# Two attention steps entered together: regrouping the window-attention units of a streaming encoder layer on one core

## The chip, the core and the metric

The kernel runs on 1 core of one Trainium2 chip. The metric is the device time of the whole program in microseconds (us), the median of a few runs. TensorE (PE) does matrix products and transposes, VectorE (DVE) and ScalarE (ACT) do elementwise work, SyncE (SP) issues nearly all DMAs from one queue in program order, and GpSimd (POOL) has almost nothing to do here.

## What is computed

One layer for a prompt of 1024 frames and a "sample" of 32 new frames: 1056 columns of tokens, cut below into eight tiles of 128 (numbers 0 to 7) and the sample (number 8, `TT`).

```python
h = rms_norm(x, norm_pre)
qa, ka, va, ga, qb, kb, vb, gb, qc, kc, vc, gc = split(h @ w_in)
oa = stick_breaking(qa, ka, va)                       # A: 12 heads, whole past
ob = band_attention(qb, kb, vb, ALiBi bias, sinks)    # B: 12 q heads, 4 kv heads, own chunk + 2 before
oc = band_attention(qc, kc, vc, relative bias)        # C: 8 heads, own chunk + 8 before
o = concat(oa * silu(ga), ob * silu(gb), oc * silu(gc)) @ w_out
x = x + rms_norm(o, norm_post)
```

## The kernel before

**Products and ticks.** `h @ w_in` is made in tiles of 128 output columns. The weights of a tile arrive in four pieces of 512 columns; ACT and DVE split each piece into a high and a low part (`w_hi`, `w_lo`), and PE takes three products of split operands (L1162, L1163, L1164, 352 token columns each). A tile is 12 groups (4 pieces by 3 token groups) of 12 matmuls. One such group is one "tick" of the plans.

**Units.** The attention is cut into 16 units of two heads: six of kind A (0 to 5), four of kind C (6 to 9), six of kind B (10 to 15; 10 to 12 share one pair of key/value heads, 13 to 15 the other). Each unit has a slot of ticks: unit 10 starts at tick 504, 11 at 528, 12 at 552 (twice as long), 13 at 600, 14 at 624, 15 at 648; the products end at tick 660, and then the output product with `w_out` (L1369 to L1375) begins.

**Steps of a B unit.** A unit handles its token tiles in five steps (`BAND_STEPS`). A step goes: scores on PE (`band_scores`, L1265) into one of two pairs of PSUM banks ("sets"); bias and row minimum on DVE (L1836), exponentials on ACT (L1540), reciprocal and scaling on DVE (L1843, L1848); the weights are transposed in blocks of 32 by DVE (L2006), sent to DRAM by SP (`part_weights`, L945) and loaded back whole (`load_weights`, L956); PE multiplies them with the values (`band_values`, L1344) into bank 7; ACT keeps the sums (L1660) and DVE multiplies them by the gate (L1770). The sample's step, and every step of the last unit 15, go another way for the transpose: PE turns them (`band_turn`, L1277) and ACT copies the result out (L1525 to L1530). Weights of a step lie in one of `B_FLIGHT` buffers `b_s`. `GROUP_END` says after which steps the sums in bank 7 are kept.

**Order.** Each engine has a plan, a list of (tick, task), sorted by the tick with Python's stable sort; entries with the same tick stay in the order in which they were appended, and products are appended first. An engine does its list in order and waits on semaphores. The ticks come from small functions: `step_starts` (scores), `values_at`, `turn_at`, `chain_at` (DVE and ACT work of a step), `cache_at`, `bias_at`. The lines that append to PE's plan:

```python
    plan = [(float(t), "product", t // 12 + 1, t % 12) for t in range(TICKS)]
...
            plan.append((START[u][i], "scores", u, i))
            if not by_blocks(u, i):
                plan.append((turn_at(u, i), "turn", u, i))
        plan += [(values_at(u, n), "values", u, n) for n in range(STEPS[kind])]
```

An "entry" below is a place where PE leaves the products for attention work and comes back; a "run" is a stretch of one kind of matmul in it (scores, values or turns). The trace has two records for each fp32 matmul of the attention, so four score matmuls are "x8" there.

Of the kernel before, what the change touches and what calls it, by code (L numbers as in the profile page):

```python
# [10 lines left out]
P = 128  # L11
# [3 lines left out]
TOK = SEQ + DEC  # L15
# [6 lines left out]
NA, NB, NC = H_A // 2, H_BKV // 2, H_C // 2  # L22
# [60 lines left out]
           step_of((6, PAST, 384), (4, PAST, 128)), step_of((5, PAST, 256), (1, 0, 256)), step_of((4, 0, PAST)), step_of((5, 0, PAST)),  # L83
           step_of((6, 0, PAST)), step_of((TT, 0, PAST + DEC))]

BAND_STEPS = {"c": ((4, 1), (5,), (3, 2), (6,), (7, 0), (TT,)), "b": ((0, 1), (2, 3), (4, 5), (6, 7), (TT,))}
GROUP_END = {"a": (3, 8, 9), "c": (1, 3, 5), "b": (1, 3, 4)}
STEPS = {"a": len(A_STEPS), "c": len(BAND_STEPS["c"]), "b": len(BAND_STEPS["b"])}
STEP0 = [sum(STEPS[UNITS[v][0]] for v in range(u)) for u in range(NU + 1)]
HEADS = 2 * (TT + 1)  # L90
# [55 lines left out]

def chain_at(u, i):

    return START[u][i] + (SECOND if UNITS[u][0] == "a" and i % 2 else 0)


def next_start(u, i):

    if i < len(START[u]):
        return START[u][i]
    if UNITS[u][0] == "b" and u + 1 < NU:
        return START[u + 1][i - len(START[u])]
    return START[u][-1] + 1.4 * (i + 1 - len(START[u]))
# [2 lines left out]

FLIGHT = 4
C_FLIGHT = 2
B_FLIGHT = 3
LAST_A, LAST_C = NA - 1, NA + NC - 1


# [7 lines left out]

def by_blocks(u, i):

    return u + 1 < NU and (UNITS[u][0] == "a" or i + 1 < STEPS[UNITS[u][0]])


def turn_at(u, i):

    kind = UNITS[u][0]
    if kind != "b":
        return chain_at(u, i) + {"a": 5, "c": 4}[kind]
    return next_start(u, i + 1) + 0.01


def values_at(u, n):

    kind = UNITS[u][0]
    if kind == "a":
        if n + FLIGHT < STEPS["a"]:
            return START[u][n + FLIGHT] - 0.02
        if n + 1 == STEPS["a"] and u < LAST_A:
            return START[u + 1][2] + 3.5
        if u < LAST_A:
            return START[u + 1][n + FLIGHT - STEPS["a"]] - 0.02
        return chain_at(u, n) + 14.6
    if kind == "c":  # L200
        if n + C_FLIGHT < STEPS["c"]:
            return START[u][n + C_FLIGHT] - 0.02
# [47 lines left out]

def pace(u, i):

    return 2.0 if UNITS[u][0] == "c" else min(2.0, 0.75 * (next_start(u, i + 1) - START[u][i]))


def at_piece(r):
# [151 lines left out]
def cache_at(u):  # L408
    return SLOT[u] + 3.0


def dve_plan():
# [27 lines left out]
def sp_plan():  # L440
    plan = [(piece_at(T, q), "piece", T, q) for T in range(1, TILES) for q in range(4)]
    for u in range(NU):
        if NEW_KV[u]:
            k, v = 12 * TILE_OF["k", u], 12 * TILE_OF["v", u]
            plan += [(k + 3.0, "store_keys", u, 0), (v + 0.6, "part_values", u, 0), (v + 8.0, "load_values", u, 0),
                     (v + 12.0, "store_values", u, 0), (cache_at(u), "cache_keys", u, 0), (SLOT[u] + (14.5 if 0 < u < NA else 10.5 if u == NA else 6.0), "cache_values", u, 0)]
# [73 lines left out]
def build(nc, x_prompt, x_sample, cache_a_k, cache_a_v, cache_b_k, cache_b_v, cache_c_k, cache_c_v,  # L520
# [3 lines left out]
    with ctx:  # L524
# [45 lines left out]
        c_bias = work[:, 3072:4352].rearrange("p (h c) -> p h c", h=2)  # L570


        oT = arena[:, 9376:9376 + TOK]

        B_HEAD = 512 + 32
        B_COLS = B_HEAD + 512
        b_s = [arena[:, 10432 + (B_COLS + 2) * i:10432 + (B_COLS + 2) * (i + 1)] for i in range(B_FLIGHT)]

        b_bias = [arena[:, c:c + 2 * n].rearrange("p (h c) -> p h c", h=2)[:, :, 0:2 * P] for c, n in ((7584, 2 * P), (8096, 672))]
# [107 lines left out]

        def part_no(u, i):

            return STEP0[u] - max(0, u - NA) + i + 1  # L690

        def parted_by(u, i):

# [112 lines left out]
        def turned_of(u, i, h):  # L806

            if UNITS[u][0] == "b":
                c = 1 + B_HEAD * h + (P if i == 0 and by_blocks(u, i) else 0)
# [53 lines left out]
        def cache_blocks(u):  # L863
            return 1 if UNITS[u][0] == "b" else 4
# [14 lines left out]
        def _(sp):  # L879
# [26 lines left out]

            def cached_values(u):
                c = P * UNITS[u][1]
                sp.dma_start(vc[:, 0:cache_blocks(u), :],
                             caches_of(u)[1][0, 0].rearrange("(b p) h d -> p b (h d)", p=P)[:, :, c:c + P]).then_inc(vc_in, 16)  # L910

            def outputs_of(u, which):
# [179 lines left out]
            for _, what, u, n in sp_plan():  # L1092
# [23 lines left out]
                elif what == "cache_keys":  # L1116

                    if u:
                        sp.wait_ge(z_ready, Z_COUNT[u - 1, STEPS[UNITS[u - 1][0]] - 1])
                    cached_keys(u)  # L1120
                elif what == "cache_values":
                    if u:
                        sp.wait_ge(pv_done, STEP0[u])
                    cached_values(u)
                elif what == "bias":
                    bias_load(u)
# [15 lines left out]
        def _(pe):  # L1142
# [139 lines left out]
            def value_rows(u, blk, h):  # L1282
                cached, own, keys = blk
                hp = slice(DH * h, DH * h + DH)

                return vc[:, cached, hp] if own is None else v_nat[KV[u] % 2][:, own, hp]

            def o_free(u, n):
                ends = GROUP_END[UNITS[u][0]]
# [157 lines left out]
        def _(act):  # L1447
# [58 lines left out]
            def turned_out(u, i):  # L1506
# [12 lines left out]
                            last.then_inc(set_free[0], 1)  # L1519
                else:  # L1520
                    z = ps[:, 512 * zb:512 * zb + 1024].rearrange("p (h k) -> p h k", h=2)
                    if i + 1 < STEPS["b"]:
# [601 lines left out]
```

## Time and profile before

| | |
|---|---|
| median of 3 runs | 1967.0 us (1963.57 to 1967.22) |
| profiled execution, its own time | 1968.51 us |
| its span | 1966.8 us |
| PE busy | 1919.5 us, 98% of the span |
| DVE busy | 1243.7 us, 63% |
| ACT busy | 657.5 us, 33% |
| mean granted clock of TensorE | 0.991 of full speed |

A busy share of 98% says that PE always has a matmul in flight, not that each of them runs at its best pitch: matmuls overlap, and what an interruption costs is seen from the distance between their starts.

### The profile page before, as it was taken

Reading aid. Unit: us, or ns where it says so; the run is one execution under the profiler, and the core shown is the slowest. Engines: PE = TensorE matmul, PEld = TensorE weight load, DVE = VectorE, ACT = ScalarE, POOL = GpSimd, SP = SyncE. Lnnn points to the kernel's source line nnn. Section 1 sums busy time; section 2 is a strip of 40 time slices with the busy share of each in tenths; the row PEclk is TensorE's granted clock in tenths of the full one; section 3 lists DMA queues with packets and bytes.
Section 4 is the critical chain, followed back from the end, with each engine's and each line's share of the span. In section 5 each row is a group of like instructions: output and inputs, shape, how many; then the busy total and the mean of one; then the engine's idle time right before and its main releaser. Section 6 shows DMA issues by size and latency. Waiting matters only on the chain.

```text
span 1966.8 us, 31027 instructions
## 1 busy us (share of the span) xinstructions
PE 1919.5 (98%) x12604; PEld 1758.3 (89%) x12604; DVE 1243.7 (63%) x2228; ACT 657.5 (33%) x1239; POOL 21.9 (1%) x66
## 2 busy tenths in 40 slices
PE   6999999999999999999999999999999999999996
PEld 5999999999999999899999999989999988888875
DVE  7358687787768778354445344555435567766898
ACT  7133343343433333122222122322223354344432
POOL 3000000000000000000000000000000000000000
PEclk9999999999999999999999999999999999999998
DMA  6447767776776767576656576555445576534476
GB/s 241 115 119 140 159 150 160 160 149 147 148 155 149 161 148 159 120 144 148 139 118 154 128 147 125 125 133 120 105 100 126 127 274 228 195 108 154 151 250 242
DMA packets 882215, 301.05 MB, mean 153 GB/s; under 512 B 618472, under 2 KB 845560, under 8 KB 880600
## 3 DMA queue, kind: packets, MB, share of 16 engines
q1 hardware_dynamic: 881912, 296.90, 61.8%
q8 instruction: 99, 1.62, 0.3%
q0 software_dynamic: 160, 2.17, 0.3%
q14 instruction: 44, 0.36, 0.1%
HBM read 210.45 MB, written 91.75 MB: 154 GB/s over the span
## 4 chain that ended last, share of the span: by engine, by line
PE 91%; DVE 5%; DMA 1%; issue 1%; SPq 1%; ACT 0%; DVEq 0%; POOL 0%
PE ps L1162 22%; PE ps L1163 21%; PE ps L1164 21%; PE ps L1373 4%; PE ps L1374 4%; PE ps L1375 4%; PE ps L1265 3%; PE ps L1344 3%; PE ps L1226 3%; PE ps L1315 3%; DVE arena L1691 1%; DVE act_lo L1698 1%; PE ps L1370 1%; PE ps L1369 1%; DMA b_out<-in_w_out_dram 0%
## 5 line engine op out<-in xcount | busy, mean ns | idle before, releaser
L1162 PE MATMUL ps<-act_hi,w_hi 128*128 128x352 f32 x2688 | 879.2, 327 | 3.9 <-DVE arena L1730 3.9
L1163 PE MATMUL ps<-act_lo,w_hi 128*128 128x352 f32 x2688 | 864.0, 321 | 0.0
L1164 PE MATMUL ps<-act_hi,w_lo 128*128 128x352 f32 x2688 | 863.8, 321 | 0.0
L1162 PEld LDWEIGHTS ps<-act_hi,w_hi 128*128 128x128 f32 x2688 | 505.6, 188 | 21.0 <-issue 18.1
L1163 PEld LDWEIGHTS ps<-act_lo,w_hi 128*128 128x128 f32 x2688 | 506.5, 188 | 0.0
L1164 PEld LDWEIGHTS ps<-act_hi,w_lo 128*128 128x128 f32 x2688 | 505.3, 188 | 0.0
L1473 ACT ACTIVATE w_hi<-w_raw 128x512 fp32r<-128x512 f32 x224 | 139.1, 623 | 343.5 <-DMA w_raw<-in_w_in_dram 343.2
L1706 DVE TENSOR_TENSOR w_lo<-w_raw,w_hi 128x512 fp32r<-128x512 f32 x224 | 150.4, 673 | 55.1 <-ACT w_hi L1473 54.8
L1540 ACT ACTIVATE arena<-arena,small 128x257 f32<-128x257 f32 (+6 forms) x180 | 101.2, 565 | 219.2 <-DVE small L1836 219.2
L2006 DVE STREAM_TRANSPOSE arena<-arena 128x1024 f32<-128x1024 f32 (+4 forms) x100 | 132.5, 1325 | 50.3 <-ACT arena L1638 49.5
L1638 ACT ACTIVATE arena<-arena 128x1024 f32<-128x1024 f32 (+1 forms) x60 | 61.0, 1017 | 250.2 <-DVE arena L1813 250.2
L1373 PE MATMUL ps<-w_hi,l_hi 128*128 128x512 f32 x280 | 110.1, 393 | 8.4 <-DVE w_lo L1890 5.5
L1375 PE MATMUL ps<-w_hi,l_lo 128*128 128x512 f32 x280 | 109.7, 392 | 0.0
L1374 PE MATMUL ps<-w_lo,l_hi 128*128 128x512 f32 x280 | 109.6, 391 | 0.0
L1836 DVE CUSTOM_DVE_ANT_0 arena<-ps,arena 128x640 f32<-128x640 f32 (+5 forms) x72 | 44.0, 660 | 93.6 <-PE ps L1265 84.2
L1789 DVE TENSOR_TENSOR arena<-ps,arena 128x1024 f32<-128x1024 f32 (+1 forms) x60 | 70.2, 1171 | 30.9 <-ACT arena L1634 30.8
L1730 DVE COPY arena<-ps 128x352 f32<-128x352 f32 x84 | 42.9, 514 | 62.0 <-PE ps L1164 61.9
L1801 DVE TENSOR_TENSOR_SCAN arena<-arena 128x512 f32<-128x512 f32 (+4 forms) x102 | 79.5, 833 | 0.8
L1548 ACT ACTIVATE w_hi<-w_raw 128x512 fp32r<-128x512 f32 x70 | 44.0, 629 | 104.1 <-DVE w_raw L1873 89.2
L1634 ACT ACTIVATE arena<-arena 128x1024 f32<-128x1024 f32 (+1 forms) x60 | 61.1, 1019 | 52.2 <-DVE arena L2016 52.2
L1630 ACT ACTIVATE arena<-ps 128x1024 f32<-128x1024 f32 (+1 forms) x60 | 58.5, 975 | 54.4 <-PE ps L1243 46.6
L1739 DVE TENSOR_SCALAR arena<-ps 128x352 f32<-128x352 f32 x48 | 25.1, 522 | 75.6 <-PE ps L1164 75.6
(173 smaller groups left out, 2086.1 us busy)
## 6 DMA issues: line engine op xcount, KB each, us to landing
w_raw<-in_w_in_dram SPq DMA_DIRECT2D x176, 256.0 KB, 3.4
weight_scratch<-arena SPq DMA_DIRECT2D x216, 128.0 KB, 3.4
arena<-weight_scratch SPq DMA_DIRECT2D x54, 512.0 KB, 4.4
b_out<-in_w_out_dram SPq DMA_DIRECT2D x80, 256.0 KB, 3.4
w_raw<-in_w_out_dram SPq DMA_DIRECT2D x70, 256.0 KB, 2.7
w_raw<-in_w_in_dram SPq DMA_DIRECT2D x96, 128.0 KB, 3.1
weight_scratch<-arena SPq DMA_DIRECT2D x80, 132.0 KB, 4.1
arena<-weight_scratch SPq DMA_DIRECT2D x40, 256.0 KB, 3.4
```

Source lines behind the costliest of these rows:

```text
L1162: mm(bank(g, GN), wh, ah, start=(k == 0), stop=False)
L1163: mm(bank(g, GN), wh, al, start=False, stop=False)
L1164: last = mm(bank(g, GN), wl, ah, start=False, stop=(k == KT - 1))
L1373: mm(out, th, wh, start=first, stop=False)
L1374: mm(out, th, wl, start=False, stop=False)
L1375: last = mm(out, tl, wh, start=False, stop=end)
L1473: fn(w_hi[:, q, :], w_raw[:, q, :], ACT.Copy).then_inc(hi_made, 1)
L1540: fn(s, s, ACT.Exp, bias=neg_max[0:rows_of(m), t:t + 1], scale=-1.0, accum_out=row_sum[0:rows_of(m), t:t + 1]).then_inc(p_exp, 1)
L1706: v.tensor_tensor(w_lo[:, slot, :], w_raw[:, slot, :], w_hi[:, slot, :].bitcast(F32), ALU.subtract).then_inc(lo_made, 1)
L1789: v.tensor_tensor(both, z, both, ALU.max).then_inc(sp_ready, 1)
L1801: v.tensor_tensor_scan(along, along, along, 0.0 if newest else carry[:, 2 * m - 8 + h:2 * m - 7 + h], ALU.add, ALU.max).then_inc(sum_ready, 1)
L2006: v.transpose(s, s).then_inc(wt_blocks, 1)
```

## The change

The B units 10 to 14 take the sample's step first and alone; the steps (0, 1) and (2, 3) start one behind the other, then (4, 5) and (6, 7). The second step of such a pair has its DVE and ACT work planned 2.7 ticks behind the first. Values are taken two steps at a time, with a fourth score buffer for it. The sums are kept after the steps 0, 2 and 4. Unit 15 keeps its single steps, but the sample is first there too. To make room, `oT` and `b_s` move, the cached values of B get their own place, one bias table lies in `mask_c`, and the loads of cached keys and values come earlier.

```diff
-BAND_STEPS = {"c": ((4, 1), (5,), (3, 2), (6,), (7, 0), (TT,)), "b": ((0, 1), (2, 3), (4, 5), (6, 7), (TT,))}
-GROUP_END = {"a": (3, 8, 9), "c": (1, 3, 5), "b": (1, 3, 4)}
+BAND_STEPS = {"c": ((4, 1), (5,), (3, 2), (6,), (7, 0), (TT,)), "b": ((TT,), (0, 1), (2, 3), (4, 5), (6, 7))}
+GROUP_END = {"a": (3, 8, 9), "c": (1, 3, 5), "b": (0, 2, 4)}
...
+def in_pairs(u):
+
+    return UNITS[u][0] == "b" and u + 1 < NU
...
-    if (kind, i, r) == ("b", 0, 0):
-        begin = 6
-    if kind == "b" and end > 24:
-
-        return [SLOT[u] + 0.5] + [SLOT[u] + 5.5 + (end - 5) * x // (n - 1) for x in range(n - 1)]
+    if in_pairs(u):
+        first, second, third = (6.5, 10.7, 16.5) if u == B0 else (0.5, 5.0, 20.0 if end > 24 else 12.0)
+        return [SLOT[u] + x for x in (first, second, second + 0.01, third, third + 0.01)]
     return [SLOT[u] + begin + (end - begin) * x // n + 0.5 for x in range(n)]
...
 def chain_at(u, i):
 
+    if in_pairs(u):
+        return START[u][i] + (2.7 if i in (2, 4) else 0)
     return START[u][i] + (SECOND if UNITS[u][0] == "a" and i % 2 else 0)
...
-B_FLIGHT = 3
+B_FLIGHT = 4
...
+    if in_pairs(u):
+        return START[u][1] - 0.04
     return next_start(u, i + 1) + 0.01
...
-    return next_start(u, n + (B_FLIGHT if n < 3 and by_blocks(u, n) else 2)) - 0.02
+    if in_pairs(u):
+        return (START[u][3] if n == 0 else START[u + 1][0 if n < 3 else 1]) - 0.02
+    return next_start(u, n + 2) - 0.02
...
-    return START[u - 2][-1] + 1.2
+    return START[u - 2][-1] + 4
```

**PE inside unit 11.** Names: `ps` is PSUM, `arena` the buffer with keys, queries, weights and values; scores are L1265 before and L1286 after, values L1344 and L1365, turns L1277 and L1298. Each line of dots stands for product groups of 12 rows (five at each place before; four, one, six and one after) or for the second half of a turn. Before, from the unit's third step to the entry that begins the next unit:

```order
L1265 MATMUL ps<-arena 128x256 x4
...
L1344 MATMUL ps<-arena 64x128 x6
L1265 MATMUL ps<-arena 128x256 x4
...
L1344 MATMUL ps<-arena 64x128 x8
L1265 MATMUL ps<-arena 32x128 x2
L1265 MATMUL ps<-arena 32x32 x2
...
L1344 MATMUL ps<-arena 64x128 x16
L1265 MATMUL ps<-arena 128x128 x2
```

After, the whole unit from its first entry:

```order
L1365 MATMUL ps<-arena 64x128 x14
L1286 MATMUL ps<-arena 32x128 x2
L1286 MATMUL ps<-arena 32x32 x2
...
L1298 MATMUL ps<-ident,arena 128x32
L1298 MATMUL ps<-ident,arena 32x32
...
L1365 MATMUL ps<-arena 64x128 x16
...
L1286 MATMUL ps<-arena 128x128 x2
L1286 MATMUL ps<-arena 128x256 x6
...
L1365 MATMUL ps<-arena 64x32 x4
...
L1286 MATMUL ps<-arena 128x256 x8
```

The scores of two steps now stand together, and so do the values; but a group of 12 products stands between the values at the second place and the scores there, and again at the third place, because these starts are whole ticks (5.0 and 12.0) and the product of the same tick is sorted ahead of the scores, the values at a hundredth of a tick less ahead of both.

**SP where unit 10 ends.** `weight_scratch` is the DRAM copy of the weights, `w_raw` a piece of `w_in`, `in_alibi_dram` and `in_attn_sinks_dram` the bias and sinks of unit 12. Before:

```order
L945 DMA weight_scratch<-arena 32x33x32 x4
L890 DMA w_raw<-in_w_in_dram 128x4x64 x2
L992 DMA arena<-in_alibi_dram 128x256
L993 DMA small<-in_attn_sinks_dram 128x1
L992 DMA arena<-in_alibi_dram 128x256
L993 DMA small<-in_attn_sinks_dram 128x1
L956 DMA arena<-weight_scratch 128x4x128 x2
```

After:

```order
L964 DMA weight_scratch<-arena 32x33x32 x4
L1011 DMA arena<-in_alibi_dram 128x256
L1012 DMA small<-in_attn_sinks_dram 128x1
L1011 DMA arena<-in_alibi_dram 128x256
L1012 DMA small<-in_attn_sinks_dram 128x1
L909 DMA w_raw<-in_w_in_dram 128x4x64 x2
L975 DMA arena<-weight_scratch 128x4x128 x2
L964 DMA weight_scratch<-arena 32x33x32 x4
L909 DMA w_raw<-in_w_in_dram 128x4x64 x2
L975 DMA arena<-weight_scratch 128x4x128 x2
```

In both the last row is the load of unit 10's last blocked step; before, PE wants it at tick 528.48, 2.4 ticks behind the load's place in the plan (526.1); after, at tick 532.98, 4.2 ticks behind its place (528.81).

**PE at the end of unit 15.** Before, the last three entries (the dots are one product group, then the second half of the turn and 18 rows of the output product):

```order
L1344 MATMUL ps<-arena 64x128 x8
L1265 MATMUL ps<-arena 32x128 x2
L1265 MATMUL ps<-arena 32x32 x2
L1277 MATMUL ps<-ident,arena 128x128 x8
...
L1344 MATMUL ps<-arena 64x128 x8
L1277 MATMUL ps<-ident,arena 128x32
...
L1344 MATMUL ps<-arena 64x32 x4
```

After:

```order
L1365 MATMUL ps<-arena 64x128 x8
L1286 MATMUL ps<-arena 128x256 x4
L1298 MATMUL ps<-ident,arena 128x128 x8
...
L1365 MATMUL ps<-arena 64x128 x8
L1298 MATMUL ps<-ident,arena 128x128 x8
...
L1365 MATMUL ps<-arena 64x128 x8
```

The last step is now the full pair of tiles (6, 7) instead of the sample, with one product group and eight value matmuls between its scores and its turn.

## Rows read from the trace of the kernel before

**Rows 1.** The page: span; busy time of PE, share, instructions.

```profile
span 1966.8 us, 31027 instructions
PE 1919.5 (98%) x12604; PEld 1758.3 (89%) x12604; DVE 1243.7 (63%) x2228; ACT 657.5 (33%) x1239; POOL 21.9 (1%) x66
```

**Rows 2.** Timeline of PE, last values of unit 10: start, us, idle before and releaser.

```profile
1296.50 1.10 PE L1344 MATMUL ps<-arena 128*64 128x128 f32 x16 [2.87 <-DMA arena<-weight_scratch]
```

**Rows 3.** Chain that ended last, in order of time: start, us, what.

```profile
1291.61 4.85 DMA arena<-weight_scratch
```

**Rows 4.** Stretches: length, busy of PE, PEld, DVE, ACT, POOL; granted clock; DMA.

```profile
1296.50:1301.20 4.70, 4.70 (x34) 3.79 (x35) 1.58 (x10) 1.67 (x10) 0.00 (x0) 0.64 0.03 7
```

**Rows 5.** Timeline of PE, an entry with scores alone.

```profile
1476.34 0.32 PE L1163 MATMUL ps<-act_lo,w_hi 128*128 128x352 f32 x1
1476.49 0.32 PE L1164 MATMUL ps<-act_hi,w_lo 128*128 128x352 f32 x1
1476.75 1.14 PE L1265 MATMUL ps<-arena 64*128 64x256 f32 x8
1477.81 0.43 PE L1162 MATMUL ps<-act_hi,w_hi 128*128 128x352 f32 x1
1478.08 0.32 PE L1163 MATMUL ps<-act_lo,w_hi 128*128 128x352 f32 x1
```

**Rows 6.** Timeline of PE, two entries with values.

```profile
1454.53 1.98 PE L1344 MATMUL ps<-arena 128*64 128x128 f32 x32
1456.44 0.93 PE L1265 MATMUL ps<-arena 64*128 64x128 f32 x8
1457.30 0.36 PE L1277 MATMUL ps<-ident,arena 32*128 32x32 f32 x4
...
1499.27 1.10 PE L1344 MATMUL ps<-arena 128*64 128x128 f32 x16
1500.30 0.47 PE L1265 MATMUL ps<-arena 64*32 64x128 f32 x8
```

**Rows 7.** Timeline of PE, scores of two A steps in one run.

```profile
336.63 2.00 PE L1226 MATMUL ps<-arena 64*128 64x512 f32 x12
338.56 0.51 PE L1243 MATMUL ps<-mask_b,ident_b 128*128 128x128 bf16 x6
```

**Rows 8.** Timeline of PE, end of unit 15 and the output product's first wait.

```profile
1598.38 1.09 PE L1277 MATMUL ps<-ident,arena 128*128 128x128 f32 x8
1599.23 0.40 PE L1162 MATMUL ps<-act_hi,w_hi 128*128 128x352 f32 x1
1601.32 1.10 PE L1344 MATMUL ps<-arena 128*64 128x128 f32 x16
1602.35 0.36 PE L1277 MATMUL ps<-ident,arena 32*128 32x32 f32 x4
...
1613.98 0.47 PE L1373 MATMUL ps<-w_hi,l_hi 128*128 128x512 f32 x1 [0.92 <-DVE w_lo L1890]
```

**Rows 9.** Timelines of PE, ACT and DVE after the scores of tiles 6 and 7 in unit 15.

```profile
1590.19 1.09 PE L1277 MATMUL ps<-ident,arena 128*128 128x128 f32 x8
...
1592.77 0.52 ACT L1540 ACTIVATE arena<-arena,small 128x257 f32<-128x257 f32 x1
...
1593.91 0.17 DVE L1843 RECIPROCAL small<-small 128x2 f32<-128x2 f32 x1 [0.40 <-ACT arena L1540]
...
1595.08 0.62 DVE L1848 TENSOR_SCALAR arena<-arena,small 128x256 f32<-128x256 f32 x2
```

**Rows 10.** A late tile copy (timeline of PE; stretch behind it), then DVE in unit 11.

```profile
817.72 0.63 PE L1162 MATMUL ps<-act_hi,w_hi 128*128 128x352 f32 x1 [3.94 <-DVE arena L1730]
...
817.70:822.00 4.30, 4.28 (x14) 3.92 (x16) 2.03 (x4) 0.00 (x0) 0.00 (x0) 0.50 0.87 128
...
1309.68 0.17 DVE L1827 COPY arena<-small 128x2 f32<-128x2 f32 x1 [4.76 <-PE ps L1265]
...
1314.20 1.28 DVE L2006 STREAM_TRANSPOSE arena<-arena 128x1056 f32<-128x1056 f32 x1
...
1319.54 0.53 DVE L1730 COPY arena<-ps 128x352 f32<-128x352 f32 x1 [3.49 <-PE ps L1164]
```

More of the change, by code:

```diff
@@ L176, in by_blocks @@
 def by_blocks(u, i):
-    return u + 1 < NU and (UNITS[u][0] == "a" or i + 1 < STEPS[UNITS[u][0]])
+    kind = UNITS[u][0]
+    return u + 1 < NU and (kind == "a" or BAND_STEPS[kind][i][0] < TT)
 def turn_at(u, i):
@@ L251, in pace @@
 def pace(u, i):
-    return 2.0 if UNITS[u][0] == "c" else min(2.0, 0.75 * (next_start(u, i + 1) - START[u][i]))
+    return 2.0 if UNITS[u][0] == "c" or in_pairs(u) else min(2.0, 0.75 * (next_start(u, i + 1) - START[u][i]))
 def at_piece(r):
@@ L404, in bias_at, with cache_values_at @@
         return unit_end_at(NA + NC - 1) + 0.3 + 0.1 * r
-    return START[u - 2][-1] + 1.2
+    return START[u - 2][-1] + 4
 def cache_at(u):
+    if UNITS[u][0] == "b":
+        return SLOT[u] - (9 if u == B0 else 20)
     return SLOT[u] + 3.0
+def cache_values_at(u):
+    if UNITS[u][0] == "b":
+        return cache_at(u) + 0.2
+    return SLOT[u] + (14.5 if 0 < u < NA else 10.5 if u == NA else 6.0)
 def dve_plan():
@@ L445, in sp_plan @@
             plan += [(k + 3.0, "store_keys", u, 0), (v + 0.6, "part_values", u, 0), (v + 8.0, "load_values", u, 0),
-                     (v + 12.0, "store_values", u, 0), (cache_at(u), "cache_keys", u, 0), (SLOT[u] + (14.5 if 0 < u < NA else 10.5 if u == NA else 6.0), "cache_values", u, 0)]
+                     (v + 12.0, "store_values", u, 0), (cache_at(u), "cache_keys", u, 0), (cache_values_at(u), "cache_values", u, 0)]
         if UNITS[u][0] != "a":
@@ L570, in build @@
         c_bias = work[:, 3072:4352].rearrange("p (h c) -> p h c", h=2)
-        oT = arena[:, 9376:9376 + TOK]
+        oT = arena[:, 8896:8896 + TOK]
+        vc_b = arena[:, 8768:8896].rearrange("p (b c) -> p b c", b=1)
         B_HEAD = 512 + 32
         B_COLS = B_HEAD + 512
-        b_s = [arena[:, 10432 + (B_COLS + 2) * i:10432 + (B_COLS + 2) * (i + 1)] for i in range(B_FLIGHT)]
-        b_bias = [arena[:, c:c + 2 * n].rearrange("p (h c) -> p h c", h=2)[:, :, 0:2 * P] for c, n in ((7584, 2 * P), (8096, 672))]
+        b_s = [arena[:, 9952 + (B_COLS + 2) * i:9952 + (B_COLS + 2) * (i + 1)] for i in range(B_FLIGHT)]
+        b_bias = [t.rearrange("p (h c) -> p h c", h=2) for t in (arena[:, 7584:8096], mask_c[:, :])]
         x_t = [arena[:, o:o + D] for o in (1152, 1152 + D, 1152 + 2 * D, 1152 + 4 * D + D // 2)]
@@ L688, in part_no @@
         def part_no(u, i):
-            return STEP0[u] - max(0, u - NA) + i + 1
+            return STEP0[u] - max(0, u - NA) + i + (UNITS[u][0] != "b")
         def parted_by(u, i):
@@ L808, in turned_of @@
             if UNITS[u][0] == "b":
-                c = 1 + B_HEAD * h + (P if i == 0 and by_blocks(u, i) else 0)
+                c = 1 + B_HEAD * h + (P if i == 1 and by_blocks(u, i) else 0)
                 return b_s[(STEP0[u] + i) % B_FLIGHT][:, c:1 + B_HEAD * h + 512]
@@ L908, in cached_values @@
                 c = P * UNITS[u][1]
-                sp.dma_start(vc[:, 0:cache_blocks(u), :],
+                sp.dma_start((vc_b if UNITS[u][0] == "b" else vc)[:, 0:cache_blocks(u), :],
                              caches_of(u)[1][0, 0].rearrange("(b p) h d -> p b (h d)", p=P)[:, :, c:c + P]).then_inc(vc_in, 16)
@@ L1118, in _ @@
                     if u:
-                        sp.wait_ge(z_ready, Z_COUNT[u - 1, STEPS[UNITS[u - 1][0]] - 1])
+                        sp.wait_ge(z_ready, Z_COUNT[u - 1, 0 if in_pairs(u - 1) else STEPS[UNITS[u - 1][0]] - 1])
                     cached_keys(u)
                 elif what == "cache_values":
-                    if u:
-                        sp.wait_ge(pv_done, STEP0[u])
+                    if u == B0:
+                        sp.wait_ge(z_ready, Z_COUNT[u - 1, STEPS["c"] - 1])
+                    elif u:
+                        sp.wait_ge(pv_done, STEP0[u - 1] + 1 if in_pairs(u - 1) else STEP0[u])
                     cached_values(u)
@@ L1284, in value_rows @@
                 hp = slice(DH * h, DH * h + DH)
-                return vc[:, cached, hp] if own is None else v_nat[KV[u] % 2][:, own, hp]
+                return (vc_b if UNITS[u][0] == "b" else vc)[:, cached, hp] if own is None else v_nat[KV[u] % 2][:, own, hp]
             def o_free(u, n):
@@ L1521, in turned_out @@
                     z = ps[:, 512 * zb:512 * zb + 1024].rearrange("p (h k) -> p h k", h=2)
-                    if i + 1 < STEPS["b"]:
+                    if BAND_STEPS["b"][i][0] < TT:
                         nk = sum(keys_of(u, m) for m in BAND_STEPS["b"][i])
```

## The prediction

> **What bounds the kernel now.** I read the page first: PE is busy for 98% of the span [rows 1], so a change pays only where PE waits, runs at the low clock, or starts its matmuls further apart than it could. Next I read PE's timeline through the B units, looking at two things: the rows that carry a wait, and the distances between starts at each entry. From unit 10 to the last product there is a single wait: the last blocked values of unit 10 stand 2.87 us for the DMA that brings their weights back from DRAM [rows 2]. The chain of waits shows that DMA in flight for 4.85 us [rows 3], and the stretch behind the wait runs at a mean granted clock of 0.64, that is partly at 1.2 GHz instead of 2.4 [rows 4]. Everywhere else in the B units PE always has work, and what is lost is lost at the joints: the product behind an entry starts late, and so does each run of another kind.
>
> **What a joint costs.** Products start 0.15 to 0.16 us apart. An entry with scores alone has 0.26 us from the last product to the first score, and 0.27 us from the first product behind it to the second [rows 5]: about 0.21 us for each entry, whatever is in it. Inside, a run has a fixed part. Eight records of scores of 256 columns take 1477.81 - 1476.75 = 1.06 us [rows 5]; the unit's first step has half of them at 128 columns and takes 0.86 us [rows 6]. So 512 columns are 0.20 us, 2048 are 0.80, and 0.26 is fixed; had 512 columns taken 0.21, it would be 0.22. I take 0.24. Values: 32 records take 1.91 us and 16 take 1.03 [rows 6], 0.055 each, which leaves 0.15 fixed. Do two steps behind one another share the fixed part? For values, yes: the 32 records are two steps. For scores the nearest row is of kind A: two steps of 2048 columns each take 1.93 us together [rows 7], 0.20 less than twice 1.06, so they shared nearly one fixed part.
>
> TensorEngine Tiling (Array Packing) of the Trainium skill, section Key Properties, says that changing the tiling mode drains TensorE. Scores are 64*128 in these rows, values 128*64 and products 128*128, so by that rule each change of kind has a price and each merge of equal kinds saves one; the rows give the price, the page none.
>
> **The change, part by part.**
>
> *Entries.* The name of the change promises three for five, which by 0.21 us would be two in each of five units. The order says otherwise. In units 11 to 14 the second and third starts are whole ticks, so a product group slips between the values and the scores: each of these units has five entries, as before. Unit 10 starts at 6.5, 10.7 and 16.5 and does get fewer. Counted from the start of the B units to the output product, entries go from 32 to 30: 2 x 0.21 = 0.4 us.
>
> *Runs.* In the same stretch score runs go from 30 to 20 and value runs from 25 to 20; turns stay at 10. That is 10 x 0.24 + 5 x 0.15 = 2.4 + 0.75 = 3.15 us. Entries and runs together 3.5 us. Bounds: 3.0 with all fixed parts at the low reading; 1.2 if scores of two steps don't share theirs; 4.4 with 0.33 for a score run ([rows 7] read with the slope of [rows 6]).
>
> *The wait at the end of unit 10.* Before, PE comes for these weights at tick 528.48, 2.4 ticks behind the load's place in SP's plan; a product group is 12 starts 0.16 apart, 1.92 us, so that is some 4.6 us, less than the 4.85 us of the DMA alone, and SP is late besides, having the bias of unit 12 ahead of it. After, the same load has 4.2 ticks (8.1 us) and two entries of about 2 us each besides; the bias stands ahead of an earlier load. The work that has to be done in this time: the second chain of the pair (bias, exponentials, scaling, transpose) is as long as in unit 11, 1315.48 - 1309.68 = 5.8 us [rows 10], and is already in the plan's 2.7 ticks plus 3. I expect no wait: 2.87 us gone, and with it the low clock: 4.70 x (1 - 0.64) = 1.69 us. Together 4.56 us. If a wait remains, the cover lost is that of SP's queue; kept whole, the gain here is nothing. All other pairs have nine or more ticks from load to use.
>
> *The fourth buffer and the moved loads.* B's cached keys and values are now asked for 9 and 20 ticks ahead of the slot, behind scores that are long done; nobody waits for them. No DMA is added, and the pieces of `w_in` behind them in SP's queue are asked for nine ticks ahead of their use. I put this at nothing.
>
> *The last unit.* Its last step is now a full one. Take the scores' end as zero. In the same step before, the turn of the previous step began at 1590.19, ACT's first exponential at +2.6, the reciprocals at +3.7, the last scaled block at +5.5 [rows 9]. PE comes for it at 1602.35 - 1598.38 = +4.0 (turn, one product group, values) [rows 8], needs 0.85 us of turning (1599.23 - 1598.38), and must wait in the middle of it: it ends at about +6.0 and not +4.8, so 1.2 us are lost. What hides it: 11 us later PE waited 0.92 us for a split piece of `w_out` [rows 8], made by DVE from DMAs that were released by the last product and not by this turn. So 0.92 of the 1.2 is taken from that wait, and 0.3 us remain. The turn and the values of the step (about 1.2 us more than the sample's) stand behind the last product now instead of before it; that only moves them. Bounds: 0, and +1.2 if the later wait moves along.
>
> **The sum**, against the profiled execution's own 1968.51 us: 1968.51 - 3.5 - 4.56 + 0.3 = 1960.75. The median of the runs is 1.5 us lower than that execution, and part of this may be a smaller wait in unit 10, which can't be gained twice; I take 1960.5 us. A measurement of this kernel tells about 0.2% (3.9 us) from no change, so the bound of "faster" is 1963.1.
>
> **The rivals.**
>
> *A. The wait stays or moves.* The loads of both pairs go through one SP queue with four transposed stores, bias and pieces ahead of them, and a DMA there has taken 4.85 us [rows 3]. If the values of the pair wait as long as before, or if the median run had little of this wait, only the joints are gained: 1967.0 - 3.5 + 0.3 = 1963.8, which is "same"; with half of it, 1962 to 1965. For it: the highest and the lowest run of before are 3.7 us apart, so something like this comes and goes. Against it: 3.5 us more plan time than before. Chance 0.22.
>
> *B. The merged runs save nothing.* If scores in another pair of banks start as a new run: 1.2 us of joints, 1968.51 - 1.2 - 4.56 + 0.3 = 1963.1. The row of the A scores [rows 7] speaks against it. Chance 0.06.
>
> *C. Slower: the pair's work on DVE delays the copies of the products.* DVE does two chains back to back, and the copy that frees the product banks (L1730, L1739) stands behind them in its queue. What that costs is seen once, elsewhere: 3.94 us of waiting and then a granted clock of 0.50 over 4.3 us [rows 10], 3.94 + 2.15 = 6.1 us at least. In unit 11 a chain is 5.8 us including 1.25 for the gate; DVE then stood idle 3.49 us before the copy [rows 10], and PE needs the bank three product groups later, 5.8 us. A second chain of 4.5 us fits into 9.3. It decides once DVE is more than 4.8 us later than this: then one such wait gives 1967, two give 1973 or more. The copies of the next tile fall right behind the second pair start in units 11, 13 and 14. Chance 0.10.
>
> *D. The joints cost nothing.* If the distance between starts came from the columns alone, merging would save nothing and the time would be 1968.51 - 4.56 + 0.3 = 1964.25. The fixed parts in the rows of the B entries [rows 5, 6] stand against it. Chance 0.02.
>
> TensorE: Matmul & The Clock Gate of the Trainium skill, section Back-to-back issue gap, gives the gap of a matmul by its columns, with no term for a change of kind; that is rival D, and the trace does not agree.
>
> **How the numbers follow.** Forecast 0.60, its own range 1957.5 to 1963. Rival A 0.22 (a quarter of it below 1963.1), B 0.06 (half), C 0.10 (a tenth of it a single short wait, which is "same"), D 0.02. Faster: 0.60 + 0.05 + 0.03 = 0.68; same: 0.17 + 0.03 + 0.01 + 0.02 = 0.23; slower 0.09. The range for 8 in 10 goes from 1957 (joints at 4.4 us, and the tail's wait fully absorbed, 2 us for chance) to 1966.5, which takes in A and B.
>
> **What the profile after will show.** Right: no wait of values for the weights' DMA near the end of unit 10 and a granted clock of 1.00 through the B units; two steps of scores in about 1.9 us instead of twice 1.06; five entries still in each of the units 11 to 14; a turn in unit 15 that stops for about 1.2 us for DVE's scaling, with a shorter first wait of the output product. Wrong: a PE wait on DVE's tile copies or on ACT's copy of the sample's turn in the B units, a wait on `weight_scratch` at another place, or score runs of 2.1 us.

## The result and the profile after

The kernel after takes 1975.7 us (median of 6 runs, 1972.49 to 1978.09), the kernel before 1965.24 us (6 runs, 1963.57 to 1967.22). The ratio is 1.0049 (95% interval 1.0039 to 1.0059): 0.5% slower, outside the range of the forecast. The profiled execution took 1976.8 us.

The page after, where [rows 1] stood for before:

```profile
span 1975.1 us, 31027 instructions
PE 1918.6 (97%) x12604; PEld 1762.2 (89%) x12604; DVE 1241.2 (63%) x2228; ACT 657.1 (33%) x1239; POOL 21.8 (1%) x66
```

PE, DVE and ACT are busy for about as long as before (1919.5, 1243.7, 657.5 us). The 8.3 us by which the span grew are idle time of PE and low clock, less what the joints saved. PE's timeline from the first B unit to the output product has these waits (start, us, instruction, idle before and releaser; before, this stretch has the single one of [rows 2] and the small ones of the output product):

```profile
1304.29 1.10 PE L1365 MATMUL ps<-arena 128*64 128x128 f32 x16 [1.58 <-DMA arena<-weight_scratch]
...
1351.43 0.47 PE L1286 MATMUL ps<-arena 64*32 64x128 f32 x8 [1.34 <-issue]
...
1431.90 0.66 PE L1183 MATMUL ps<-act_hi,w_hi 128*128 128x352 f32 x1 [3.53 <-DVE arena L1748]
...
1517.53 0.75 PE L1286 MATMUL ps<-arena 64*32 64x128 f32 x8 [4.07 <-issue]
...
1576.96 0.47 PE L1286 MATMUL ps<-arena 64*32 64x128 f32 x8 [1.31 <-issue]
...
1611.51 0.44 PE L1298 MATMUL ps<-ident,arena 128*128 128x128 f32 x2 [0.27 <-DVE arena L1869]
...
1612.48 0.88 PE L1298 MATMUL ps<-ident,arena 128*128 128x128 f32 x6 [0.54 <-DVE arena L1869]
```

The 64*32 scores at 1351, 1517 and 1577 us are the sample's step, the first of units 12, 14 and 15. "<-issue" says only that the profile found no semaphore for the wait. The stretches behind the two long waits (same columns as [rows 4]):

```profile
1517.53:1524.00 6.47, 6.47 (x28) 6.41 (x29) 2.62 (x10) 2.57 (x7) 0.00 (x0) 0.51 0.36 72
1431.90:1435.20 3.30, 3.30 (x12) 3.30 (x12) 1.55 (x3) 0.61 (x1) 0.00 (x0) 0.52 0.59 89
```

**The balance.** Waits: 1.58 + 1.34 + 3.53 + 4.07 + 1.31 + 0.27 + 0.54 = 12.64 us. Low clock: 6.47 x 0.49 + 3.30 x 0.48 = 4.75 us. Before, the same stretch lost 2.87 + 1.69 = 4.56 us [rows 2, 4]. That makes 12.83 us more. From unit 10's first scores to the first output product is 1602.64 - 1250.80 = 351.84 us before and 1613.11 - 1251.70 = 361.41 after: 9.57 more, and 10.2 for equal work, since the full step's values (0.67 us longer than the sample's) now stand behind that product. So 12.83 - 10.2 = 2.6 us were saved at the joints. Unit 10 begins 0.90 us later than before, and the stretch behind the first output product is 2.2 us shorter: 0.90 + 9.57 - 2.2 = 8.3.

**What the sample's scores wait for.** SP, then ACT, then DVE, ahead of 1351.43:

```profile
1335.87 0.96 SPq L1011 DMA_DIRECT2D mask_c<-in_alibi_dram  x1
...
1339.19 0.93 SPq L975 DMA_DIRECT2D arena<-weight_scratch  x2
1340.22 4.64 SPq L964 DMA_DIRECT2D weight_scratch<-arena  x4
1344.90 2.27 SPq L909 DMA_DIRECT2D w_raw<-in_w_in_dram  x2
...
1349.11 0.63 ACT L1494 ACTIVATE w_hi<-w_raw 128x512 fp32r<-128x512 f32 x1 [12.63 <-DMA w_raw<-in_w_in_dram]
...
1342.71 0.53 DVE L1760 TENSOR_SCALAR arena<-ps 128x352 f32<-128x352 f32 x1 [2.98 <-PE ps L1185]
1349.77 0.69 DVE L1727 TENSOR_TENSOR w_lo<-w_raw,w_hi 128x512 fp32r<-128x512 f32 x1 [6.53 <-ACT w_hi L1494]
1350.38 0.95 DVE L1760 TENSOR_SCALAR arena<-ps 128x352 f32<-128x352 f32 x2
```

Read it backwards. The scores start as soon as DVE has copied the last two thirds of the query tile (L1760, 1350.38 to 1351.33). These copies stand behind the split of a piece of `w_in` (L1727). The split waits for ACT's, ACT's for the DMA of the piece, and SP asked for the piece at 1344.90, behind the four stores of the pair's second step (4.64 us), the load of the pair's first step, and the four bias loads. DVE is idle for 6.53 us, ACT for 12.63. The other two waits of this kind have the same rows (the piece comes to ACT at 1515.21 and 1574.64). At 1431.90 it is the copies of a value tile (L1748, transposes) that stand behind the split, and with them PE's next product bank:

```profile
1425.55 0.51 DVE L1748 STREAM_TRANSPOSE arena<-ps 128x352 f32<-128x352 f32 x1
1430.69 0.69 DVE L1727 TENSOR_TENSOR w_lo<-w_raw,w_hi 128x512 fp32r<-128x512 f32 x1 [4.64 <-ACT w_hi L1494]
1431.30 0.97 DVE L1748 STREAM_TRANSPOSE arena<-ps 128x352 f32<-128x352 f32 x2
```

In the kernel before, SP at the same place has one step's stores, then the piece (timeline of SP):

```profile
1338.65 3.38 SPq L945 DMA_DIRECT2D weight_scratch<-arena  x4
1342.07 2.36 SPq L890 DMA_DIRECT2D w_raw<-in_w_in_dram  x2
1345.61 0.92 SPq L956 DMA_DIRECT2D arena<-weight_scratch  x2
```

The two kernels reach the same tick at different times, so these starts can't be compared as they stand. Unit 12's first entry is a common mark. It begins with values, at 1348.33 us after and, before, here:

```profile
1352.96 1.98 PE L1344 MATMUL ps<-arena 128*64 128x128 f32 x32
```

Before, the piece is asked for 1352.96 - 1342.07 = 10.9 us ahead of that entry; after, 1348.33 - 1344.90 = 3.4 us ahead. It is 7.5 us later.

**Unit 10's wait.** The chain of waits of the kernel after that ends in the 1.58 us:

```profile
1291.85 0.51 SPq L975
...
1293.01 0.44 SPq L964
...
1294.72 2.05 SPq L964
...
1296.82 3.69 DMA weight_scratch<-arena
...
1300.53 0.37 SPq L975
...
1300.93 3.31 DMA arena<-weight_scratch
...
1304.29 1.10 PE ps L1365 x16
```

From one load's issue to the next (1291.85 to 1300.53) 8.7 us pass: four stores, their landing, the load. A pair needs this twice, one behind the other, and then the landing. No engine's arithmetic is in that chain.

### The profile page after: what moved, and what is told of

It reads as the page before. It is cut to its first block, busy times and chain, and to the rows that moved or that the text cites. A ratio compares the mean times of both kernels' runs of the same rounds, so it can differ in the third digit from the quotient of the medians.

```text
span 1975.1 us, 31027 instructions
## 1 busy us (share of the span) xinstructions
PE 1918.6 (97%) x12604; PEld 1762.2 (89%) x12604; DVE 1241.2 (63%) x2228; ACT 657.1 (33%) x1239; POOL 21.8 (1%) x66
## 4 chain that ended last, share of the span: by engine, by line
PE 87%; DVE 6%; SPq 2%; DMA 2%; issue 2%; ACT 1%; DVEq 0%; POOL 0%; ACTq 0%
PE ps L1183 21%; PE ps L1184 20%; PE ps L1185 20%; PE ps L1394 4%; PE ps L1396 4%; PE ps L1395 4%; PE ps L1286 3%; PE ps L1365 3%; PE ps L1247 3%; PE ps L1336 3%; SPq L964 1%; PE ps L1391 1%; PE ps L1390 1%; DMA weight_scratch<-arena 1%; PE ps L1173 0%
## 5 line engine op out<-in xcount | busy, mean ns | idle before, releaser
L1727 DVE TENSOR_TENSOR w_lo<-w_raw,w_hi 128x512 fp32r<-128x512 f32 x224 | 150.8, 674 | 118.5 <-ACT w_hi L1494 118.2
L1561 ACT ACTIVATE arena<-arena,small 128x257 f32<-128x257 f32 (+7 forms) x180 | 101.3, 565 | 220.7 <-DVE small L1857 220.7
L1760 DVE TENSOR_SCALAR arena<-ps 128x352 f32<-128x352 f32 x48 | 24.8, 522 | 73.8 <-PE ps L1185 73.7
```

Of the source, the lines that this page charges most:

```text
L1561: fn(s, s, ACT.Exp, bias=neg_max[0:rows_of(m), t:t + 1], scale=-1.0, accum_out=row_sum[0:rows_of(m), t:t + 1]).then_inc(p_exp, 1)
L1727: v.tensor_tensor(w_lo[:, slot, :], w_raw[:, slot, :], w_hi[:, slot, :].bitcast(F32), ALU.subtract).then_inc(lo_made, 1)
```

## The experiments

All ran beside the kernel before on the same chip; a ratio is to that one, with its 95% interval.

**1. The piece ahead of the second step's stores**

```diff
+late = 0.4 if in_pairs(u) and i == 4 else 0
-plan += [(at, "part_weights", u, i), (at + (2.6 if u >= B0 else 4.0), "load_weights", u, i)]
+plan += [(at + late, "part_weights", u, i), (at + (2.6 if u >= B0 else 4.0), "load_weights", u, i)]
```

> The changed kernel, with the stores of each pair's second step planned 0.4 ticks later in SP's queue, so that the next piece of w_in is issued ahead of them. Queue theory (the four stores hold SP, the piece of w_in lands late, DVE's split waits for it and the copies of the query tile queue behind the split): the three waits of the sample's scores in units 12, 14 and 15 (1.34, 4.07, 1.31 us) and the low clock behind the second (3.4 us of loss) go, the time falls from 1975.7 to about 1966; the waits at 1304 us (1.58) and 1432 us (3.53) stay. Rival, DVE overworked: DVE does the same work, the waits stay, 1975. Rival, transfers collide: the same bytes move, the piece is as late as before, 1973 to 1976.

Measured: 1972.61 us, ratio 1.003 (1.0018 to 1.0042). The three waits of the sample's scores are gone, but waits of 3.79 us for unit 10's weights and 3.38 us at a value tile stand in the trace, both with a stretch of low clock behind them. The sample's turns in units 12 and 14 wait too, 0.42 and 1.40 us, so the time stayed 6.6 us above the expectation. The pieces were what the sample's scores waited for; what stands behind the pieces is late now.

**2. DVE's copies ahead of the late split**

```diff
-plan = [(piece_at(T, q) + 4.2, "lo", T, q) for T in range(1, TILES) for q in range(4)]
+plan = [(piece_at(T, q) + (5.95 if q == 1 and 12 * (T - 2) >= SLOT[B0] else 4.2), "lo", T, q) for T in range(1, TILES) for q in range(4)]
```

> The changed kernel, SP's queue as it is; on DVE the split of the second piece of each tile stands behind the three copies of the tile before, from unit 10 on. Queue theory: the piece is as late as before, but nothing queues behind it, so the three waits of the sample's scores go, about 1966 us. DVE overworked: the copies come when the chains are done, the waits stay, 1975. If the late piece itself were what PE lacks, a wait on w_lo would take their place and the time would stay near 1975.

Measured: 1967.37 us, ratio 0.9998 (0.9989 to 1.0008). This one number gives back 8.3 us by the medians. SP's list is that of the kernel after, and yet the waits at 1351, 1431, 1517 and 1577 us are gone or at 0.20 us; two turns of the sample wait instead, 0.32 and 0.59 us, since the split is later still. Left is the wait for unit 10's weights:

```profile
1306.10 1.97 PE L1365 MATMUL ps<-arena 128*64 128x128 f32 x16 [4.03 <-DMA arena<-weight_scratch]
```

**3. The cached loads later**

```diff
-        return SLOT[u] - (9 if u == B0 else 20)
+        return SLOT[u] - 9
```

> The changed kernel, with the cached keys and values of unit 13 asked for 9 ticks ahead of the slot instead of 20. If these five DMAs, right behind the eight that store new keys, make the piece of w_in in unit 12 late, the wait of 3.53 us at 1432 us and the low clock behind it (1.7 us) go: 1970.5. If the wait comes from the chains of the pair alone, it stays: 1975.7. The three waits of the sample's scores stay in both cases.

Measured: 1974.45 us, ratio 1.0034 (1.0021 to 1.0046). The wait at the value tile fell from 3.53 to 1.30 us, the sample's waits stayed (1.68, 4.39 and 0.49 us). The clock behind it was at 1.00, where the kernel after has 3.30 us at 0.52. So the moved loads, which I had put at nothing, were about 2.2 us of that one wait and the 1.6 us of low clock behind it. The total fell by only 1.3 us, inside the intervals; unit 10's wait was 3.43 us in this profile, against 1.58 in that of the kernel after.

**4. The kernel before, with its bias loads behind the load of the weights**

```diff
-    return START[u - 2][-1] + 1.2
+    return START[u - 2][-1] + 2.0
```

> The kernel before, with only the bias load of each B unit 0.8 ticks later, so that in unit 10 it stands behind the load of the last weights in SP's queue. If that wait (2.87 us, and 1.7 us of low clock behind it) is SP's lateness, the load goes out 1.9 us earlier, the wait shrinks to about 1 us and the clock stays up: 1.9 to 3.6 us faster than before, 1962 to 1963.5. If the DMA's own time sets it, 1965.2 as before.

Measured: 1963.14 us, ratio 0.9982 (0.9973 to 0.9991). No wait is left in the B units. Unit 10's wait of [rows 2] came from four small loads (1.9 us of issue) ahead of the load, and one number in the kernel before takes it away. The change promised this gain by other means and didn't get it.

**5. The pairing alone undone**

```diff
+        if u > B0:
+            step = (SLOT_LEN[u] - 5.0) / 4
+            return [SLOT[u] + 0.5] + [SLOT[u] + 4.98 + step * x for x in range(4)]
...
-        return START[u][i] + (2.7 if i in (2, 4) else 0)
+        return START[u][i] + (2.7 if i in (2, 4) and u == B0 else 0)
```

> The kernel after, with the pairing alone undone in units 11 to 14: the sample's step stays alone and first and the buffers stay as they are, but the four full steps start one at a time, 4.75 ticks apart (10.75 in unit 12), and their DVE and ACT work isn't shifted. Theory (SP's queue): the stores of two steps stand behind one another on SP only because the steps are paired. Spread out, the stores leave room for the pieces of w_in, so the three waits of the sample's scores (0.47 to 1.34, 4.07, 1.31 us in the kernel after) shrink to less than a third, with the low clock at 1517 us; the price is 8 more score runs, 8 x 0.24 = 1.9 us. About 1975.7 - 6.7 - 3.4 + 1.9 = 1967.5 us. Rival (the sample's place): it is the sample's step at the head of the unit that is wrong, since it needs the last of the three tile copies half a tick behind the last product; then the three waits stay and the time is 1975.7 + 1.9 = 1977.6 us.

Measured: 1965.35 us, ratio 0.9996 (0.9987 to 1.0005). The three waits and the one at 1431 us are gone, though the sample is first in its unit as in the kernel after. Unit 10, whose pairs this run keeps, still waits 2.51 us for its weights. SP's timeline before unit 12 shows why the others are gone: the piece now stands behind the stores of one step, at 1337.42, 10.6 us ahead of the unit's first entry (1348.06 in this run), and not behind two rounds, at 1344.90. The copies don't wait.

```profile
1334.03 3.34 SPq L967 DMA_DIRECT2D weight_scratch<-arena  x4
1337.42 2.27 SPq L912 DMA_DIRECT2D w_raw<-in_w_in_dram  x2
1340.41 0.92 SPq L978 DMA_DIRECT2D arena<-weight_scratch  x2
1341.38 1.06 SPq L912 DMA_DIRECT2D w_raw<-in_w_in_dram  x2
1343.38 3.56 SPq L967 DMA_DIRECT2D weight_scratch<-arena  x4
```

The rival, the sample's place by itself, is out, and so are the moved buffers, which this run keeps.

**6 and 7. The change mended, and then without ties.** Number 6 is number 2 with `bias_at` at +9 instead of +4. Number 7 adds

```diff
-        first, second, third = (6.5, 10.7, 16.5) if u == B0 else (0.5, 5.0, 20.0 if end > 24 else 12.0)
+        first, second, third = (6.5, 10.7, 16.5) if u == B0 else (0.5, 4.98, 19.98 if end > 24 else 11.98)
```

> The kernel after with two edits of DVE's and SP's order: the split of the second piece planned behind the three tile copies (as in e2_copies_first), and the bias loads asked for 5 ticks later (START[u - 2][-1] + 9), which takes them out of the chain of stores and loads at the end of unit 10. Theory: SP's chain there becomes shorter by the four bias loads, 1.3 + 3.3 = 3 to 4 us of queue before the first pair's load; the wait at the weights of unit 10's end (4.03 us in e2_copies_first, and its low clock of 3.4 us) falls to under 1 us: 1967.4 - 3.4 - 3.4 = 1960.6 to 1964 us. Rival: the chain is bound by the landings of store and load, not by the issue; then nothing moves and it stays at 1967.4 us.

> m1_mended with the starts of the pairs a fiftieth of a tick earlier (4.98, 11.98, 19.98 instead of 5.0, 12.0, 20.0), so that no product group slips between the values and the scores, and a unit of 11 to 14 has three entries and not five. Theory of the joints: 8 entries fewer at 0.21 us, 1.7 us faster than m1_mended. Rival (an entry has no price of its own, only its runs): no difference. Second rival: the scores come 1.9 us earlier and values too, so one of the waits comes back; slower.

Measured: 1962.49 us, ratio 0.9983 (0.9974 to 0.9992), and 1961.51 us, ratio 0.9975 (0.9965 to 0.9984). Unit 10's wait fell from 4.03 to 2.10 us, not to under 1: with the bias out of the way the loads are issued only 1.8 us (1292.78 to 1291.02) and 2.5 us earlier, because the landings stay. A wait of 1.12 us at 1430.73 is for a split itself (`w_lo`, L1727): this piece is late for its own product, since SP asks for it behind eight stores of new keys, the five cached loads and now the bias loads too. In number 7 the two waits are 1.99 and 0.79 us. Number 7 was 1.0 us faster; the intervals overlap, so its gain rests on the profiles. In the two profiles the stretch from unit 10's first scores to the output product is 1598.52 - 1250.28 = 348.24 us and 1597.60 - 1250.33 = 347.27 us. Number 7 waits 0.44 us less there, but has this stretch behind its wait, where number 6 has the full clock:

```profile
1303.33:1307.80 4.47, 4.47 (x33) 3.38 (x33) 1.38 (x9) 1.51 (x6) 0.00 (x0) 0.62 0.35 80
```

That is 4.47 x 0.38 = 1.7 us of low clock. Cleared of both, the eight entries gave 0.97 - 0.44 + 1.7 = 2.2 us, where 8 x 0.21 = 1.7 was expected.

**8. The same two edits in the kernel before**

```diff
-    return START[u - 2][-1] + 1.2
+    return START[u - 2][-1] + 2.0
...
-plan = [(piece_at(T, q) + 4.2, "lo", T, q) for T in range(1, TILES) for q in range(4)]
+plan = [(piece_at(T, q) + (5.95 if q == 1 and 12 * (T - 2) >= SLOT[B0] else 4.2), "lo", T, q) for T in range(1, TILES) for q in range(4)]
```

> The kernel before with the same two edits in its own form: bias loads 0.8 ticks later (as in e4_before_bias), and the split of the second piece planned behind the three tile copies from unit 10 on. Theory: in the kernel before nothing in the B units waits for a tile copy, so the copies' place is worth nothing there and the time is that of e4_before_bias, 1963.1 us. Rival: the copies' place is a gain of its own, whatever the grouping; then it is clearly below 1963 us, down to 1960.

Measured: 1962.1 us, ratio 0.9979 (0.9971 to 0.9988), against 1963.14 us of number 4: the same within the intervals. The copies' place is worth 8 us with the pairs and about nothing without them.

**9. The kernel before, with late pieces alone**

```diff
-plan = [(piece_at(T, q), "piece", T, q) for T in range(1, TILES) for q in range(4)]
+plan = [(piece_at(T, q) + ({1: 3.8, 2: 0.9}.get(q, 0) if 12 * (T - 2) >= SLOT[B0] else 0), "piece", T, q) for T in range(1, TILES) for q in range(4)]
```

> The kernel before with one thing of the change alone: from unit 10 on, SP asks for the second piece of a tile of w_in 3.8 ticks (7.3 us) later, as late as it came in the kernel after, and for the third 0.9 ticks later. Nothing else is moved. Theory (it takes both, the late split and work that waits for the copies behind it): here the sample is last in its unit, the first step of a unit needs the first of the three tile copies, which stands ahead of the split, so the three waits of 1.3 to 4.1 us don't come; only a wait at a tile whose copies are longer, like that of 3.53 us at 1431.90, may. 1966 to 1971 us. Rival (late pieces are enough): waits at most unit starts and then at the products, as in the kernel after: 1974 us or more, since here 12 pieces are late and not four.

Measured: 1990.29 us, ratio 1.0123 (1.0106 to 1.014). My expectation fell and the rival's held: late pieces are enough (12 of them here, against four that mattered in the kernel after, and shifted from a list that SP already did late). They don't need the sample at the head of the unit; here it is the product banks that come free late, as at 1431 us after. The run doesn't say what pieces only as late as those after would have cost with the sample last; three of the four waits there were the sample's scores at the head of a unit. Two of the eight waits, and DVE's rows ahead of the first:

```profile
1267.42 0.43 PE L1162 MATMUL ps<-act_hi,w_hi 128*128 128x352 f32 x1 [3.47 <-DVE arena L1730]
...
1503.54 0.43 PE L1162 MATMUL ps<-act_hi,w_hi 128*128 128x352 f32 x1 [3.53 <-DVE arena L1730]
...
1264.47 0.69 DVE L1706 TENSOR_TENSOR w_lo<-w_raw,w_hi 128x512 fp32r<-128x512 f32 x1 [6.88 <-ACT w_hi L1473]
...
1266.85 0.52 DVE L1730 COPY arena<-ps 128x352 f32<-128x352 f32 x1
```

**10. Late pieces, copies first.** Number 9 with the edit of number 2.

> p1_before_late_pieces with one edit: DVE's split of the second piece is planned behind the three tile copies from unit 10 on (as in e2_copies_first). The pieces arrive as late as before, 25 us of loss in p1_before_late_pieces. Theory (a late piece costs only through what is queued behind its split on DVE): the seven waits for tile copies go, and the time is that of the kernel before, 1964 to 1968 us, with the wait at unit 10's weights left. Rival (the piece is late for its own product as well, or ACT's work behind its split is what is late): waits for w_lo or for the values of ACT come in their place, and it stays over 1975 us.

Measured: 1973.1 us, ratio 1.0035 (1.0021 to 1.0049), between the two expectations. 17 of the 25 us go with the copies' place. No wait for `w_lo` came. Most of what stays is the neighbour on SP: the shifted pieces stand ahead of the load of unit 10's weights.

```profile
1301.83 1.98 PE L1344 MATMUL ps<-arena 128*64 128x128 f32 x16 [6.43 <-DMA arena<-weight_scratch]
```

A smaller part is what the rival's second half named. PE still waits for tile copies three times (0.90, 0.99 and 0.29 us). At the first, the copies on DVE stand behind scaling that waits for exponentials, and these stand on ACT behind ACT's own half of the late split:

```profile
1265.37 0.63 ACT L1473 ACTIVATE w_hi<-w_raw 128x512 fp32r<-128x512 f32 x1 [10.39 <-DMA w_raw<-in_w_in_dram]
1265.90 0.50 ACT L1540 ACTIVATE arena<-arena,small 128x257 f32<-128x257 f32 x1
...
1267.02 0.17 DVE L1843 RECIPROCAL small<-small 128x2 f32<-128x2 f32 x1 [4.84 <-ACT arena L1540]
...
1268.73 0.52 DVE L1730 COPY arena<-ps 128x352 f32<-128x352 f32 x1
```

**11 and 12. Unit 11's pairs later, and the cached loads too.** Number 11 is number 7 with the starts 6.98 and 12.98 in unit 11; number 12 adds the edit of number 3.

```diff
-        first, second, third = (6.5, 10.7, 16.5) if u == B0 else (0.5, 4.98, 19.98 if end > 24 else 11.98)
+        first, second, third = (6.5, 10.7, 16.5) if u == B0 else (0.5, 6.98, 12.98) if u == B0 + 1 else (0.5, 4.98, 19.98 if end > 24 else 11.98)
```

> m3_mended_no_ties with the pairs of unit 11 alone two ticks and one tick later (6.98 and 12.98 instead of 4.98 and 11.98), and with them the values of unit 10's last two steps two ticks (3.8 us) later. In m3_mended_no_ties PE waited 1.99 us for their weights and then ran at half its clock for 2.9 us. Theory (a fixed serial chain of stores, landings and loads on SP, about 9 us per step): the weights land when they did, so the wait and its low clock go: 1.99 + 1.3 = 3.3 us faster, 1958.2 us. Rival: SP's chain moves along with unit 11's work, and the wait stays; no difference.

> m4_unit_11_later with the loads of cached keys and values of unit 13 asked for 9 ticks ahead of its slot instead of 20 (as in e3_cache_later). In m3_mended_no_ties a wait of 0.79 us was left at 1431 us, behind a piece that SP had asked for after eight store and four load DMAs. Theory: the wait goes, 0.8 us faster than m4_unit_11_later. Rival: something else on SP takes its place there (it did in part in e3_cache_later); no difference.

Measured: 1959.03 us, ratio 0.9969 (0.9958 to 0.9981), and 1957.99 us, ratio 0.9963 (0.995 to 0.9975). The wait for unit 10's weights is gone in number 11, and that at 1428 us (1.29 us there) in number 12, whose B units run through. The times of numbers 7, 11 and 12 alone don't separate them, since neighbouring intervals overlap; the waits in the traces do. Number 12 from unit 10 to the last turn (columns as in [rows 4]):

```profile
1250.98:1592.10 341.12, 340.70 (x2468) 327.00 (x2467) 185.50 (x573) 113.47 (x334) 0.00 (x0) 1.00 0.56 132
```

Number 12 is the best kernel of the study: 7.2 us faster than before and, by the medians of different occasions, 17.7 us faster than the kernel after, with the same regrouping and five edits of plan numbers. The kernel before, mended too (number 8), is 4.1 us behind it; they ran on different occasions, and their intervals overlap at the edge.

One more order wasn't tried: both steps' stores ahead of the first load. The load waits for a count of landed stores that the second step's stores raise as well, so it would need a semaphore of its own.

## Why the prediction was wrong

**The step that failed** is that of the fourth buffer and the moved loads: "No DMA is added, and the pieces of `w_in` behind them in SP's queue are asked for nine ticks ahead of their use. I put this at nothing." The pieces are planned nine ticks ahead, but SP does its list in order, and a pair puts two rounds of stores, landing and load behind one another. Ahead of unit 12 SP issues three such loads at 1329.46, 1339.19 and 1348.22 us, 9.7 and 9.0 us apart. The piece planned for tick 546 (the group of tick 552 starts 1.92 us before the values at 1348.33, and six groups more are 11.5 us: about 1334.9 us) was asked for at 1344.90, 3.4 us ahead of unit 12's first entry and not 10.9 as before. It still came in time for its own product; the work queued behind its split on DVE did not. I had counted how far ahead of its use a DMA is planned and not who stands behind the instruction that waits for it. The four waits that numbers 2 and 5 took away are 1.34 + 3.53 + 4.07 + 1.31 = 10.25 us, and with the 4.75 us of low clock 15.0 us: more than the whole loss. Against the sum of 1960.75 us the profiled execution was 16.05 us longer; these 15.0 and the 1.58 us left in unit 10 account for it, and the smaller terms come to half a us the other way. At the wait of 3.53 us the moved loads had the larger part: number 3 took away 2.2 us of it by their place alone.

**Unit 10's wait** (4.56 us forecast as gained) came out at 1.58 us without low clock in this execution: 3.0 us gained. In numbers 1 to 3, with the same plan for unit 10 or nearly so, it was 3.4 to 4.0 us with low clock behind it, so on the whole nothing like 4.56 us was gained. The sentence "After, the same load has 4.2 ticks (8.1 us) and two entries of about 2 us each besides" counted time up to PE and left SP's chain out: 8.7 us for a step and 3.3 to land. The clause on lost cover ("that of SP's queue; kept whole, the gain here is nothing") named the right queue and gave it no weight. Rival A had the mechanism for this place.

**The joints** (3.5 us): 2.6 us by the balance above, inside the bounds of 1.2 and 4.4. Two steps' scores in one run took 1.93 us, as forecast:

```profile
1323.29 2.00 PE L1286 MATMUL ps<-arena 64*128 64x256 f32 x16
1325.22 0.43 PE L1183 MATMUL ps<-act_hi,w_hi 128*128 128x352 f32 x1
```

Number 12 confirms the size where nothing disturbs it. From unit 10's first scores to the first output product it takes 342.72 us, with 0.67 for equal work and without the turn's 0.81, 342.58; number 8 takes 1597.02 - 1249.64 = 347.38. That is 4.8 us for 10 entries, 10 score runs and 5 value runs, priced at 2.1 + 2.4 + 0.75 = 5.25. Rivals B and D are out. That units 11 to 14 keep five entries was right, and mending it gave what it was priced at.

**The last unit** (0.3 us): the turn waited 0.27 + 0.54 = 0.81 us, not 1.2, and the output product's first waits (0.92 us [rows 8], and 0.69 us ten us later) are gone, so this part came out as a small gain.

**Rival C** (0.10) had the right victim, the tile copies on DVE, but the wrong cause: it asked whether DVE would be busy for 4.8 us more. DVE was idle; it stood at a split whose piece was late. It priced a wait at 6.1 us with its low clock; the two long ones cost 5.1 and 7.2 us, the two short ones 1.3 us each. Its test could never have found this, since it read DVE's work and not what heads DVE's queue.

**What stays open.** Whether the lateness after would have cost anything with the sample last, as said under number 9. And why SP's stores take as long as they do: four stores took 3.3 to 5.2 us on SP in the rows shown and in others, and no run shows what that time is made of.

## What to carry to other kernels

When steps are grouped, draw the queue that all their transfers go through, with issue and landing of each round in series, before counting what the compute engines save: here the grouping saved 2.6 us of joints and cost 15.0 us until the queues were put in order, and then saved 4.8. An instruction that waits for a prefetched transfer should not stand ahead of something urgent on its engine if the transfer can slip; that it is early enough for its own use is no protection. And a slower version may be a good change with stale plan numbers: look for the waits and move one number at each before throwing it away.

## What the runs showed of the hardware

A late DMA whose own product never waited for it still cost time: in number 9, 12 pieces asked for 7.3 us later (and 12 more 1.7 us later) cost 25 us, of which putting the urgent copies first gave back 17.

Waits of PE of 1.31, 1.34 and 1.58 us left the clock at 1.00. Behind waits of 3.53 and 4.07 us it was at 0.52 over 3.30 us and at 0.51 over 6.47 us. Waits of 2.0 to 2.5 us went both ways: 2.10 us (number 6) and 2.51 us (number 5) left it at 1.00; behind 1.99 us (number 7) it was at 0.62 over 4.47 us, and behind 2.34 us (number 9) at 0.66 over 3.31 us.

At the low clock products started 0.29 us apart and not 0.32, twice the 0.16 of the full one, so a stretch costs a little less than its length times the missing clock:

```profile
1432.65 0.49 PE L1185 MATMUL ps<-act_hi,w_lo 128*128 128x352 f32 x1
1432.94 0.49 PE L1183 MATMUL ps<-act_hi,w_hi 128*128 128x352 f32 x1
```
